# Two transformer-like blocks on one core: four gate products put ahead of the delta rule's z products, and norm sums that end with two squares on TensorE

## The reference, cut to what matters

```
xn = rmsnorm(h, norm_mix)
(dq, dk, dv, dz, da, db, aq, ak, av, gate_dn, gate_da) = split_columns(xn @ w_in, ...)
o_dn = deltanet_branch(dq, dk, dv, dz, da, db, ...)      # ends: rmsnorm(o, out_norm) * silu(dz)
o_da = dilated_attention_branch(aq, ak, av, rel_bias)
merged = sigmoid(gate_dn) * (o_dn @ w_branch_dn) + sigmoid(gate_da) * (o_da @ w_branch_da)
h = h + merged @ w_out
rmsnorm: x * rsqrt(mean(x * x over 1024 features) + eps) * g
```

## Time and profile before

| | us |
|---|---|
| median of 3 runs | 4089.5 (4086.95 to 4093.19) |
| profiled execution, its own time | 4082.31 |
| its span, first to last instruction | 4080.5 |
| TensorE matmuls busy | 3818.6 (94%), 23037 instructions |
| TensorE weight loads busy | 3308.2 (81%) |
| VectorE / ScalarE / GpSimd busy | 2399.2 / 1682.2 / 739.6 |
| mean granted TensorE clock | 0.973 |

### The profile page before, as it was taken

The page is one execution under the profiler, slowest core; times in us unless marked ns, Lnnn a source line. Parts: engine busy times, 40 slices in busy tenths (PEclk is TensorE's granted clock), DMA queues, the critical chain, the costliest instruction groups (busy, mean ns, idle before and its releaser), DMA issues. The chain is left out here.

```text
span 4080.5 us, 57384 instructions
## 1 busy us (share of the span) xinstructions
PE 3818.6 (94%) x23037; PEld 3308.2 (81%) x23037; DVE 2399.2 (59%) x4212; ACT 1682.2 (41%) x2809; POOL 739.6 (18%) x582
## 2 busy tenths in 40 slices
PE   8999989989888879999999999997999999799998
PEld 5788767777787879999999999775777877677887
DVE  6455323447879767777777777556643345674333
ACT  4523332444456883333333333436532233554222
POOL 0112000253104513222233222201000010101000
PEclk9999999989999999999999999998999999899999
DMA  5211334433345459888888887321143432202332
GB/s 206 69 40 43 112 132 176 166 97 92 111 144 166 163 187 307 292 278 285 284 275 287 278 289 226 119 69 52 54 134 114 144 124 89 63 30 83 97 94 78
DMA packets 209193, 617.30 MB, mean 151 GB/s; under 512 B 18464, under 2 KB 68640, under 8 KB 205088
## 3 DMA queue, kind: packets, MB, share of 16 engines
q1 hardware_dynamic: 168352, 465.76, 35.2%
q0 software_dynamic: 40576, 147.87, 10.4%
HBM read 583.67 MB, written 29.88 MB: 150 GB/s over the span
## 5 line engine op out<-in xcount | busy, mean ns | idle before, releaser
L510 DVE TENSOR_TENSOR wlo<-raw,whi 128x1024 fp32r<-128x1024 f32 x576 | 714.7, 1241 | 704.8 <-ACT whi L502 704.2
L544 PE MATMUL ps<-hhi,whi 128*128 128x512 f32 (+1 forms) x2824 | 1075.2, 381 | 12.3 <-ACT uact L3372 8.9
L546 PE MATMUL ps<-hlo,whi 128*128 128x512 f32 (+1 forms) x2824 | 1049.2, 372 | 0.4 <-DVE hlo L2609 0.4
L502 ACT ACTIVATE whi<-raw 128x1024 fp32r<-128x1024 f32 x660 | 693.4, 1054 | 605.4 <-PE ps L555 455.6
L555 PE MATMUL ps<-hhi,wlo 128*128 128x512 f32 (+1 forms) x2824 | 663.2, 373 | 0.0
L544 PEld LDWEIGHTS ps<-hhi,whi 128*128 128x128 f32 x2824 | 533.1, 189 | 115.3 <-issue 22.7
L546 PEld LDWEIGHTS ps<-hlo,whi 128*128 128x128 f32 x2824 | 533.4, 189 | 68.9 <-issue 3.6
L555 PEld LDWEIGHTS ps<-hhi,wlo 128*128 128x128 f32 x2824 | 511.5, 188 | 72.1 <-issue 4.8
L544 PE MATMUL ps<-ag_hi,whi 128*128 128x384 f32 x1024 | 342.1, 334 | 0.0
L546 PE MATMUL ps<-ag_lo,whi 128*128 128x384 f32 x1024 | 342.0, 334 | 0.0
L510 POOL TENSOR_TENSOR wlo<-raw,whi 128x1024 fp32r<-128x1024 f32 x85 | 209.2, 2468 | 328.9 <-ACT whi L502 328.0
(11 more groups left out here) (629 smaller groups left out, 6160.2 us busy)
## 6 DMA issues: line engine op xcount, KB each, us to landing
raw<-w_in SPq DMA_DIRECT2D x151, 512.0 KB, 3.7
raw<-peer_u SPq DMA_DIRECT2D x128, 512.0 KB, 4.6
raw<-peer_v SPq DMA_DIRECT2D x128, 512.0 KB, 4.3
raw<-w_mod SPq DMA_DIRECT2D x96, 512.0 KB, 3.7
raw<-w_gate SPq DMA_DIRECT2D x66, 512.0 KB, 3.6
raw<-w_up SPq DMA_DIRECT2D x66, 512.0 KB, 3.5
raw<-w_down SPq DMA_DIRECT2D x66, 512.0 KB, 3.5
gate_dram<-stage SPq DMA_DIRECT2D x24, 1024.0 KB, 4.7
```

What stands on the lines that cost most here:

```text
L502: a.x.activation(whi[n % NW][:], raw[i % NRAW][:], ACT.Copy, bias=0.0, scale=1.0).then_inc(*a.gives("hi", i))
L510: e.x.tensor_tensor(wlo[n % NW][:], raw[i % NRAW][:], whi[n % NW][:].bitcast(F32), ALU.subtract).then_inc(*e.gives(*lo_sig(i)))
L544: t.x.matmul(o, w, p.hi, start=grp.opens and k == 0, stop=False)
L546: t.x.matmul(o, w, p.lo, start=False, stop=False)
```

## The change

Two edits. First, the units of gate blocks 0 and 1 (dn and da, four slabs) stand ahead of the four z units in the list; the drain of the dilated items comes after eight units instead of four. The first four gate outputs get buffers of their own in memory that the second chain used, and wait for the last `unit_t` instead of the last dilated output. The modulation blocks are spread among the units that are left, two fewer. Second, in every norm sum GpSimd stops one block earlier, and TensorE multiplies the last two squares itself.

```diff
@@ sum_gpsimd @@
-        elif c < KC - 1:
+        elif c < KC - 2:
             g.wait_ge("sum_g", use, c - 1)
             g.x.tensor_tensor(nm.acc[:], nm.acc[:], nm.sq[c % 2][:], ALU.add).then_inc(*g.gives("sum_g", use, c))
@@ sum_tensor @@
-        t.wait_ge("sum_g", use, KC - 2)
+        t.wait_ge("sum_g", use, KC - 3)
         t.x.matmul(o, ones[:], nm.acc[:], start=True, stop=False)
-        t.wait_ge("sum_a", use, KC - 1)
-        t.x.matmul(o, ones[:], nm.sq[(KC - 1) % 2][:], start=False, stop=True).then_inc(*t.gives("sum_t", use))
+        for c in (KC - 2, KC - 1):
+            t.wait_ge("sum_a", use, c)
+            ins = t.x.matmul(o, ones[:], nm.sq[c % 2][:], start=False, stop=c == KC - 1)
+        ins.then_inc(*t.gives("sum_t", use))
@@ gate buffers @@
     gate = [sb(f"gate{i}", WK + 82 + 2 * i, [T]) for i in range(6)]
+    gate_first = [sb(f"gate_first{i}", WK + kb, [T]) for i, kb in enumerate((62, 64, 66, 60))]
     def gate_buffer(which, o):
-        return gate[(2 * o + "dn da".split().index(which)) % 6]
+        i = 2 * o + "dn da".split().index(which)
+        return gate[i % 6] if o >= 2 else gate_first[i]
@@ gate_scalar @@
-        if o >= 3:
+        if o < 2:
+            a.wait_ge("unit_t", 3)
+        elif o < 5:
+            a.wait_ge("da_v", "oda", 3, 3)
+        else:
             a.wait_ge("merge_v", "lo" if which == "dn" else "sum", o - 3)
-        else:
-            a.wait_ge("da_v", "oda", 3, 3)
@@ ctxnorm_tensor @@
-        yield coming("clate", ("sum_g", "c0mix", KC - 2), ("sum_a", "c0mix", KC - 1))
+        yield coming("clate", ("sum_g", "c0mix", KC - 3), ("sum_a", "c0mix", KC - 1))
@@ spine @@
-    spine += ... + coupled(u_da[-12:], m0[16:32]) + u_z + u_merge[:2]
-    spine += coupled(u_merge[2:] + u_out[:6], m0[32:] + m1[:16]) + u_out[6:]
+    spine += ... + coupled(u_da[-12:], m0[16:32]) + u_merge[:4] + u_z
+    spine += coupled(u_merge[4:] + u_out[:6], m0[32:] + m1[:16]) + u_out[6:]
@@ order @@
     run(36)
-    run(4)
+    run(8)
     plan.drain("dilated")
     plan.put("do", "xres")
-    run(24)
+    run(20)
```

More of the change, by code:

```diff
@@ L3568, in program @@
     m0, m1 = mods
-    spine += u_dn[:2] + coupled(u_dn[2:], m0[:16]) + u_da[:-12] + coupled(u_da[-12:], m0[16:32]) + u_z + u_merge[:2]
-    spine += coupled(u_merge[2:] + u_out[:6], m0[32:] + m1[:16]) + u_out[6:]
+    spine += u_dn[:2] + coupled(u_dn[2:], m0[:16]) + u_da[:-12] + coupled(u_da[-12:], m0[16:32]) + u_merge[:4] + u_z
+    spine += coupled(u_merge[4:] + u_out[:6], m0[32:] + m1[:16]) + u_out[6:]
     spine += cm0.units[:6] + mixed(cm0.units[6:], u_wq[:NWQ]) + u_wq[NWQ:] + u_cout + cnet.units + cm1.units + u_peer
```

## The result

| | median us (runs) | lowest to highest | ratio to before, 95% interval |
|---|---|---|---|
| before | 4090.44 (18) | 4086.95 to 4095.34 | |
| change | 4082.99 (18) | 4075.03 to 4090.12 | 0.9977, 0.9971 to 0.9984 |

The change makes the kernel faster by 0.23%: 9.4 us by the ratio, 6.5 to 11.9 by its interval, and 7.5 between the medians. The forecast was 4084.5, with 0.68 on "within 0.2%" and 0.26 on "faster by more".

What follows compares the result with a forecast made beforehand. TensorE paces the kernel (matmuls busy 94%), so time moves where it idles. Drain -11.7, residual +7.3, norm sums -0.6 sum to -5.0 from the 4089.5 median: 4084.5 us, range over the cases 4075.5 to 4092.

Steps and rivals of the forecast that it cites:

- The likeliest case: The forecast itself: drain won, part given back at the residual, 4084.5 us, own range 4081 to 4088, chance 0.55.
- The drain is won: Dilated items woven into eight gate and z products end by 600, some 4 us to spare; gain 11.7 us.
- 17.8 us pass without slab work: TensorE's stretch from the fourth z product's end, 576.69, to the first gate product, 594.51, in before's profile.
- weaving: Placing dilated items among the four added products was charged 0.5 us per two products, 1.0 in all.
- ScalarE's table loads at nothing: Four Sigmoids among the Exps were taken to cost 0; bounds 0 and four more loads, 5.1 us of ScalarE.
- Given back at the residual: After the fourth z product (T), slab loads queue behind the residual: waits 6.3 us, low clock 1.0, 7.3 lost.
- the rival by which the loads slip past it: Slab loads after z do not queue behind the residual, so the whole gain stands: -12.3, 4077.2 us, chance 0.22.
- The blocks' places: 16 blocks of modulation slabs lie among 26 products instead of 28, with 0.7 us of slack for a load.
- crowded: Loads over 0.7 us later stall some eight close pairs of modulation blocks: ends at +8, 4097 us, chance 0.11.
- Norm sums: Ten sums lose a GpSimd add and gain a TensorE product: -0.6 us, bounds -2 and +3.
- block1's sum: Between the chain's and the next norm's first product, at low clock, added work was charged 0.5 us.
- The sum: -11.7 + 7.3 - 0.6 = -5.0 us, giving 4084.5 when taken from the median of 4089.5.

Runs made afterwards that it cites:

- the three kernels that take the residual out of the way: The change with residual transfers spread (ratio to before 0.9965), with modulation blocks two products later (0.9958), or with spread residual and a block before `w_out` (0.9945).
- before again: The kernel before, unchanged, run and profiled a second time: median 4089.41 us, ratio 1.0001 to before.
- the gates alone: Gate slabs moved as in the change, norm sums left as in the kernel before: median 4082.39 us, ratio 0.9986 to before.

## Why the prediction was nearly right

The likeliest case was the one that happened, and its sign and mechanism held: 4084.5 was forecast, 4083.0 measured. The measured 9.4 is more than the 5.0 of the forecast's sum, and just beyond the 8.2 within which I had put 0.68 of the chance; the medians look closer than the sum because before's median over 18 runs is 4090.4 and not the 4089.5 that I subtracted from. Step by step:

*The drain is won.* Right. The items end by 603.6, within the eight products, but with 1.8 us to spare and not 4 (their last scores start at 590.8, or 589.5 without this execution's lateness, where 588 was forecast), and no idle time stands on TensorE from 546 on. The eight products end at 605.40, or 604.1 without the 1.3 that this execution was late by at 534 (604.1 in the second profile too); 604.6 was forecast, so weaving cost 0.5 and not 1.0. But **"17.8 us pass without slab work" was the term mis-sized most**: in two other executions with the drain it is 20.3 and 20.4. Before's second gate product ends at 605.65, in these two at 608.8 and 608.6 (less what they were late by), in the mean 607.7; with the two products that the change has done more by then, the gain is 607.7 - 604.1 + 10.9 = 14.5. Forecast: 11.7. From before's first profile alone it would be 12.4.

*ScalarE's table loads at nothing.* Right for the time. The whole kernel has two table loads more (81 for 79, 2.6 us of ScalarE), halfway between the bounds of none and four. Eight or nine lie between 546 and 606 (seven in before), and TensorE waited for nothing there.

*Given back at the residual.* The mechanism was right row by row, and the rival by which the loads slip past it fell. The residual goes out at T + 1.45 as forecast, the wait for the fourth modulation slab is 3.63 (forecast 4.2), the da product starts at T + 13.7 (13.9). The clock was under-charged: 1.0 in the forecast, and the product behind the stall alone lost 8.41 - 5.45 = 3.0 in one profile of the change and 1.3 in the other. By the table, 14.5 - 6.1 = 8.4 are given back, and the three kernels that take the residual out of the way are 7.4, 8.9 and 8.6 ahead of the others at the first merge. Forecast: 7.3, its wait nearly exact, its clock too small. The Trainium skill (DMA: Bandwidth & Descriptors, Queues, rings and completion order) says that each DMA engine takes a queue's descriptors in ring order; the trace agrees, since the residual's eight transfers landed 2.7 to 5.3 us after their issues, so by 615.4, and the slab issued behind them at 610.54 became usable only at 616.68.

*The blocks' places.* The rival "crowded" (+8) did not come: no wait of a matmul for a transfer stands between 620 and 780. What I did not see is the opposite, a place left bare: no block ahead of the first `w_out`, 3.33 of wait for 1.23 and the low clock behind it, 4.9 us against a kernel with a block there and its slab split earlier. Against before it costs nothing net, by chance: the wait for `msb` near 683 (1.55, 2.32 and 1.19 in the three profiles with the drain) is gone, and the gain is 6.1 at the second row as at the first.

*Norm sums.* -0.6 was forecast, with bounds -2 and +3; the run with these alone gives -1.6 to +5.7 and can't tell. One part has the wrong sign. The forecast charged 0.5 for block1's sum and left out that the chain's sum just ahead of it waited 4.0 for its accumulator `chacc`. That wait is gone. Over the two sums together (slab splits from 2494 to 2614) the seven kernels with the new sums gain 0.80 to 1.06 on before's first profile, and the two others without them, before again and the gates alone, differ from it by at most 0.03. This is the one place where the traces show a gain of the norm sums clear of spread.

*The sum.* 14.5 - 8.4 = 6.1 by the traces, 11.7 - 7.3 = 4.4 by the forecast for the same, and 9.4 (6.5 to 11.9) by the timing. The two terms were too small by 1.1 and 2.8, on opposite sides, which left the forecast closer than its terms, and that is luck. The 3 us between traces and timing are not located. Part is that few executions were profiled: before's two took 4.4 more in the mean than the change's two (spans 4085.6 and 4081.2), while the medians of 18 lie 7.5 apart.

## What to carry to other kernels

When work moves out of an idle stretch, look at what else had been using that stretch for free, here eight transfers in the queue that also feeds the products; put them in pieces behind loads that are already needed. A list that is spread evenly over another has places that matter: when its length changes, look at each dependency that a spread element had covered, not at the average density. And take the size of a drain from more than one execution when the clock falls in it.

## What the runs showed that I had not expected

The low clock after a stall is not one size. After the same waits in the same kernel the drain was 17.8 us in one execution and 20.3 in another, with granted clocks of 0.68 and 1.00 against 0.52 and 0.79 in its two windows. In the change the product behind the stall of 3.63 took 8.4 us (matmuls of 0.63 where 0.39 is usual); in the change's second profile, after a stall of 3.90, it took 6.7. So one execution differed from another of the same kernel by 1.7 to 2.5 us at such a place.

A residual of eight transfers of 256 KB, issued over 3.65 us, held back a slab of 512 KB issued right behind it until 6.1 us after that slab's own issue; it was usable 9.8 us after the first of the eight had gone out, and from 610 to 620 the DMA engines were 98% busy at 368 GB/s. With the burst cut into pieces placed beside dense work, the same load was in time.
